# A chunk's triangular system solved in two steps of 64 tokens, without the last level of the inverse

## What is computed

```python
def _wkv_step(S, inp):
    r, w, k, v, a, b = inp
    sa = jnp.einsum('bhvk,bhk->bhv', S, a)
    S = S * w[:, :, None, :] + sa[..., None] * b[:, :, None, :] + v[..., None] * k[:, :, None, :]
    return S, jnp.einsum('bhvk,bhk->bhv', S, r)
...
S_T, y = lax.scan(_wkv_step, wkv0.astype(jnp.float32),
                  (tm(r), tm(decay), tm(k), tm(v), tm(-kk), tm(kk * a)))
```

## Time and profile before

| | before |
|---|---|
| median of the runs | 3294.47 us |
| span of the profiled execution | 3295.0 us |
| TensorE busy (products) | 3173.8 us, 96% |
| VectorE busy | 1845.3 us, 56% |
| ScalarE busy | 1332.7 us, 40% |
| GpSimd busy | 1201.8 us, 36% |
| mean granted TensorE clock | 0.991 |
| chunk stage, chunks 0 to 7 | about 1870 to 2402 us |
| one chunk of 1 to 6 | 66.5 us |

### The profile page before, as it was taken

The page is one execution under the profiler, slowest core; times in us unless marked ns, Lnnn a source line. Parts: engine busy times, 40 slices in busy tenths (PEclk is TensorE's granted clock), DMA queues, the critical chain, the costliest instruction groups (busy, mean ns, idle before and its releaser), DMA issues.

```text
span 3295.0 us, 69900 instructions
## 1 busy us (share of the span) xinstructions
PE 3173.8 (96%) x25744; PEld 2881.1 (87%) x25744; DVE 1845.3 (56%) x3147; ACT 1332.7 (40%) x2785; POOL 1201.8 (36%) x841
## 2 busy tenths in 40 slices
PE   8999999999999999999999999999999999999998
PEld 5688887787999999997899887878788899999998
DVE  3466663226444478857303377777744644458885
ACT  2244445512544533322213365565521355443332
POOL 0000000010766777721222222223223276677771
PEclk9999999999999999999999999999999999999999
DMA  3122224500544544422213201110152154554442
GB/s 113 43 79 65 71 74 147 180 13 20 159 155 157 187 138 137 139 96 75 84 53 114 99 14 34 33 40 27 29 179 45 50 161 158 158 186 141 140 140 77
DMA packets 306260, 330.39 MB, mean 100 GB/s; under 512 B 54350, under 2 KB 287745, under 8 KB 305954
## 3 DMA queue, kind: packets, MB, share of 16 engines
q1 hardware_dynamic: 300178, 308.64, 29.6%
q0 software_dynamic: 5904, 19.21, 1.8%
HBM read 232.05 MB, written 116.16 MB: 106 GB/s over the span
## 4 chain that ended last, share of the span: by engine, by line
PE 72%; DVE 8%; PEld 6%; issue 4%; POOL 3%; ACT 2%; SPq 2%; DMA 1%; DVEq 0%; PEldq 0%; ACTq 0%; POOLq 0%
PE bank L651 69%; PEld bank L651 6%; PE bank L659 4%; DVE arena L3605 1%; SPq L1769 1%; POOL wloA L2085 1%; DVE hT L3676 1%; POOL arena L2085 1%; POOL wloS L2085 1%; SPq L1710 0%; SPq L1764 0%; DVE arena L3058 0%; DVE arena L3622 0%; DVE arena L3166 0%; DVE fb L3310 0%
## 5 line engine op out<-in xcount | busy, mean ns | idle before, releaser
L651 PE MATMUL bank<-arena 128*32 128x128 f32 (+19 forms) x7390 | 947.8, 316 | 35.5 <-DVE hT L3676 12.9
L651 PEld LDWEIGHTS bank<-arena 128*128 128x128 f32 (+9 forms) x7390 | 734.8, 165 | 220.4 <-issue 36.8
L2302 ACT COPY arena<-bank 128x512 f32<-128x512 f32 (+14 forms) x527 | 235.0, 484 | 633.1 <-PE bank L651 430.4
L2085 POOL TENSOR_TENSOR arena<-arena 128x512 f32<-128x512 f32 x120 | 164.8, 1373 | 599.2 <-PE bank L651 366.9
L2525 ACT ACTIVATE whiS<-arena 128x512 fp32r<-128x512 f32 x180 | 113.0, 628 | 406.2 <-POOL arena L2085 390.7
L2085 POOL TENSOR_TENSOR wloA<-arena,whiA 128x512 fp32r<-128x512 f32 x180 | 261.4, 1466 | 13.4 <-ACT whiA L2522 13.4
L2085 POOL TENSOR_TENSOR wloS<-arena,whiS 128x512 fp32r<-128x512 f32 x180 | 238.7, 1340 | 49.1 <-ACT whiS L2525 49.1
L3471 DVE TENSOR_TENSOR hT<-hT,bank 128x536 f32<-128x536 f32 x280 | 197.6, 706 | 80.9 <-PE bank L651 80.4
L659 PE MATMUL bank<-table,arena 128*128 128x128 f32 (+5 forms) x1422 | 180.0, 268 | 29.1 <-DVE arena L3178 13.1
L651 PE MATMUL bank<-hiT,whiS 128*128 128x268 f32 x768 | 199.9, 288 | 5.3 <-DVE loT L3310 3.7
L3315 DVE TENSOR_TENSOR arena<-std,bank 128x268 f32<-128x268 f32 x192 | 80.4, 432 | 217.6 <-PE bank L651 206.3
(11 more groups left out here) (320 smaller groups left out, 8536.4 us busy)
## 6 DMA issues: line engine op xcount, KB each, us to landing
u_scratch<-arena SPq DMA_DIRECT2D x480, 134.0 KB, 1.8
arena<-in_ffn_w_up SPq DMA_DIRECT2D x64, 512.0 KB, 4.1
arena<-u_scratch SPq DMA_DIRECT2D x56, 536.0 KB, 5.0
arena<-in_ffn_w_down SPq DMA_DIRECT2D x112, 256.0 KB, 4.3
arena<-u_scratch SPq DMA_DIRECT2D x56, 402.0 KB, 5.9
arena<-past_scratch SPq DMA_DIRECT2D x32, 640.0 KB, 7.2
past_scratch<-in_cache_kv_latent SPq DMA_DIRECT2D x128, 128.0 KB, 2.4
past_scratch<-in_cache_k_rope SPq DMA_DIRECT2D x128, 32.0 KB, 2.2
```

The source lines that it names most:

```text
L651: return pe.matmul(out, lhsT, rhs, start=first, stop=last, skip_group_check=group)
L2085: return pool.tensor_tensor(out, a, b, op)
L2302: lane.do(act.copy(dst, b if view is None else view(b)), ring.drained)
```

## The change

The inverse stops at blocks of 64 tokens, so `level_64` and its three copies go. `solved` takes the place of `level_64`, `first_sums` and the first product of `finals`. It sums the right-hand side of the upper 64 tokens in one bank (`top`) and that of the lower 64 in another (`low`), solves the upper 64 with the upper block of XT, subtracts their part from the lower right-hand side by further products into `low`, and solves the lower 64. ScalarE copies P1 and SA each in two halves of 64 partitions, four copies in a row. On TensorE the filler `keep_busy` ahead of three steps goes, `key_sums` and `before(1)` move behind the upper solve, and one `keep_busy(rv)` stands behind the correction. On ScalarE `norms` and `deviations` (first half) and `diagonals` (second half) now stand behind all four copies.

```diff
+                def solved(d, fillers):
+                    upper, lower = slice(0, RN), slice(RN, P)
                     s_b.wait(pe, c)
-                    b = ra.bank()
+                    low = ra.bank(ahead=2)
+                    top = ra.bank(free=True)
                     for k in range(4):
-                        mm(b[:, k * P:(k + 1) * P], ar[:, 4 * d + k, 0, :], Sm[:, 4 * d + k, :], k == 0, False, True)
+                        for rows, out in ((upper, top), (lower, low)):
+                            mm(out[rows, k * P:(k + 1) * P], ar[:, 4 * d + k, 0, rows], Sm[:, 4 * d + k, :], k == 0, False, True)
+
+                    def value_sums(rows, out, depth, last):
+                        for j in range(8):
+                            h = 8 * d + j
+                            ins = mm(out[rows, j * RN:(j + 1) * RN], NR[0:depth, j * 2 * P + rows.start:j * 2 * P + rows.stop],
+                                     v[0:depth, h * RN:(h + 1) * RN], False, last and j == 7, True)
+                        return ins
+
+                    ra.done(value_sums(upper, top, RN, True))
+                    top_at = ra.filled.n
+                    value_sums(lower, low, P, False)
+                    b = narrow(ra, top_at)
+                    for j in range(8):
+                        ins = mm(b[upper, j * RN:(j + 1) * RN], XT[upper, j * P:j * P + RN], P1[upper, j * RN:(j + 1) * RN], True, True)
+                    ra.done(ins)
+                    fillers[0]()
+                    apart(ra.drained, ra.filled.value())
                     for j in range(8):
                         h = 8 * d + j
+                        ins = mm(low[lower, j * RN:(j + 1) * RN], ma[upper, h * P + RN:(h + 1) * P], SA[upper, j * RN:(j + 1) * RN],
+                                 False, j == 7, True)
                     ra.done(ins)
+                    low_at = ra.filled.n
+                    fillers[1]()
+                    b = narrow(ra, low_at)
+                    for j in range(8):
+                        ins = mm(b[lower, j * RN:(j + 1) * RN], XT[lower, j * P + RN:(j + 1) * P], P1[lower, j * RN:(j + 1) * RN], True, True)
+                    ra.done(ins)
 ...
                 def finals(d, taken, stated):
-                    keep_busy(ra)
-                    ra.wait_drained()
-                    b = ra.bank()
-                    for j in range(8):
-                        ins = mm(b[:, j * RN:(j + 1) * RN], XT[:, j * P:(j + 1) * P],
-                                 P1[:, j * RN:(j + 1) * RN], True, True)
-                    ra.done(ins)
                     sa_at = ra.filled.n
 ...
-                level_64(0, ma, [when(prepare, lambda: key_sums(c + 1, wn)), lambda: first_sums(0), nothing])
+                solved(0, [when(prepare, lambda: key_sums(c + 1, wn)), lambda: keep_busy(rv)])
 ...
-                level_64(1, ma, [nothing, lambda: first_sums(1), when(prepare, lambda: before(1))])
+                solved(1, [when(prepare, lambda: before(1)), lambda: keep_busy(rv)])
 ...
+            def rows_out(dst, rows, scale=1.0):
                 b = ring.bank()
+                lane.do(act.activation(dst[rows, :], b[rows, :], ACT.Copy, scale=scale), ring.drained)
+
+            def solved(others):
+                upper, lower = slice(0, RN), slice(RN, P)
+                rows_out(P1, upper)
+                rows_out(SA, upper, -1.0)
+                others()
+                rows_out(P1, lower)
+                rows_out(SA, lower, -1.0)
 ...
-                take_turned()
-                take_w_64()
+                solved(lambda: None)
                 if prepare:
                     norms(c + 1, wn)
                 if finish:
                     deviations(c - 1, P)
-                take(P1, P, 512)
-                take_x_64()
-                negated(SA, P, 512)
 ...
-                take_turned()
+                solved(lambda: None)
                 if wn == TAIL:
                     diagonals_tail()
                 elif prepare:
                     diagonals(c + 1, MA[1 - par])
-                take_w_64()
-                take(P1, P, 512)
-                take_x_64()
-                negated(SA, P, 512)
```

More of the change, by code:

```diff
@@ L1416, in level_32 @@
                 ra.done(ins)
-            def level_64(d, ma, fillers):
-                crossed_at = ra.filled.n
-                fillers[2]()
-                keep_busy(ra)
-                b = narrow(ra, crossed_at)
-                for j in range(8):
-                    ins = turn(b[0:64, j * 64:(j + 1) * 64], XT[0:64, j * P:j * P + 64], 64)
-                ra.done(ins)
[L1427 to L1440, removed]
@@ L1442, in chunk @@
             def chunk(c, par, nth, finish=True, prepare=True, wn=P):
                 ar, v, ma = AR[par], vt[par], MA[par]
-                def first_sums(d):
+                def solved(d, fillers):
+                    upper, lower = slice(0, RN), slice(RN, P)
                     s_b.wait(pe, c)
-                    b = ra.bank()
+                    low = ra.bank(ahead=2)
+                    top = ra.bank(free=True)
                     for k in range(4):
-                        mm(b[:, k * P:(k + 1) * P], ar[:, 4 * d + k, 0, :], Sm[:, 4 * d + k, :], k == 0, False, True)
+                        for rows, out in ((upper, top), (lower, low)):
[14 more added lines that the diff above has]
+                    fillers[0]()
+                    assert ra.filled.n == top_at + 1
+                    apart(ra.drained, ra.filled.value())
@@ L1452, in first_sums @@
                     for j in range(8):
                         h = 8 * d + j
-                        ins = mm(b[:, j * RN:(j + 1) * RN], NR[:, j * 2 * P:j * 2 * P + P],
-                                 v[:, h * RN:(h + 1) * RN], False, j == 7, True)
+                        ins = mm(low[lower, j * RN:(j + 1) * RN], ma[upper, h * P + RN:(h + 1) * P], SA[upper, j * RN:(j + 1) * RN],
+                                 False, j == 7, True)
+                    ra.done(ins)
+                    low_at = ra.filled.n
@@ L2836, in take_x_32 @@
                 lane.do(ins, ring.drained)
-            def take_turned():
-                take(XW6[0:64, :], 64, 512)
-            def take_w_64():
+            def rows_out(dst, rows, scale=1.0):
                 b = ring.bank()
[L2843 to L2847, removed]
+                lane.do(act.activation(dst[rows, :], b[rows, :], ACT.Copy, scale=scale), ring.drained)
[6 more added lines that the diff above has]
+                rows_out(SA, lower, -1.0)
             def key_factors(c, w):
```

## The result

| | before | after |
|---|---|---|
| median of the runs | 3294.95 us (4 runs) | 3382.32 us (4 runs, 3381.07 to 3384.50) |
| ratio to before, 95% interval | | 1.0263 (1.0248 to 1.0277) |
| span of the profiled execution | 3295.0 us | 3382.7 us |
| mean granted TensorE clock | 0.991 | 0.971 |
| full chunk | 66.5 us | 78.5 us |

What follows compares the result with a forecast made beforehand. VectorE's chain, almost level with TensorE's, has only 1.1 us slack per chunk, which decides. Six full chunks at 7.9 + 3.8 give 70, chunk 0 +3.7, chunk 7 +5: +79 on 3294.5, so 3373.5 us; range 3322 to 3396.

Steps and rivals of the forecast that it cites:

- A: The forecast itself: late diagonals, GpSimd collisions and the lower clock together, 3373 us; chance 0.50.
- TensorE's path: Solve steps after each half's last `level_32` product: the split solve lets TensorE's state product start 2.3 us earlier per half.
- Rival D: Half-width pairs don't overlap in the columns and lower value sums cost 1.90: 26 us more, 3400; chance 0.11.
- (a) diagonals: Second half, ScalarE: `diagonals` behind four copies starts `low_inverses` 11.65 us after the last `level_32` product, not 5.5.
- (b) roots: First half, ScalarE: `norms` and `deviations` behind SA lower leave 0.8 of TensorE's 2.3 us gain at `new_taken`.
- (c) GpSimd of the sum: Late group norm on GpSimd blocks VectorE's additions and scan: first half's last `level_32` product to second-half masks, 21.9 becomes 24.5.
- Rival C: Neither GpSimd collisions nor lower clock: +4.5 us per chunk, 3328 us; chance 0.13.
- The clock: Lower TensorE clock for about 5 us behind each of two idle times per chunk: +3.8 us per chunk.
- Rival B: Fillers hold the clock up or its cost is hidden under the masks: 3349 us; chance 0.17.
- Rival E: TensorE's path sets the end, VectorE's does not: 2.3 us gained in each of 16 halves, 3258 us; chance 0.06.

Runs made afterwards that it cites:

- e6: The kernel before, with only ScalarE's `diagonals` in the second half moved behind the copy of SA: 3370.7 us, ratio 1.0223.
- e5: The changed kernel in its own order, with GpSimd's group norm cut to 16 of 1024 columns: 3336.6 us, ratio 1.0120.
- e4: The changed kernel with 13 and 8 more filler products in TensorE's two long idle times per chunk: 3356.5 us, ratio 1.0190.
- e8: The kernel before without the three fillers per half that the change removes: 3335.6 us, ratio 1.0127.
- e1: The changed kernel with the second half's order undone (`before(1)` ahead of the solve, `diagonals` behind the copy of P1 upper): 3359.3 us, ratio 1.0191.
- e3: The changed kernel with the order of both halves undone (`diagonals`, `norms` and `deviations` early), split solve kept: 3342.8 us, ratio 1.0143.

## Why the prediction was right

Forecast 3373.5, measured 3382.3, in the range; the mechanism was the forecast one (A). By its steps, with the numbers of the chunk shown above:

- *TensorE's path.* State sums 1.09 (said 1.1), lower value sums as the 64x64 ones, SA at X + 8.6 (8.8). Rival D falls with them. One term was wrongly put at nothing, though it is small: the changes between 64-row and 128-row products do cost. In the trace of after, single products with 64 columns start 0.06 us apart within a group and 0.15 where the shape changes, so each of the four changes in a half takes about 0.1 us.
- *(a) diagonals.* `low_inverses` at Q + 11.5 (11.65), Q to L 23.4 (23.4). e6 isolates it.
- *(b) roots and (c) GpSimd of the sum.* `new_taken` at X + 12.5 (12.8), M at X + 24.1 (24.5). The order in which the two engines take turns was the one forecast, and the scan does wait. It took 3.24 us, against 2.28 in e5. Rival C falls. The page SBUF — State Buffer of the Trainium skill (section Who interferes with whom) says that a VectorE instruction with two SBUF inputs contends with a GpSimd instruction that reads SBUF; by these two numbers that holds for the scan too.
- *The clock.* L to X 15.4 (13.5 + 1.9), M to Q 15.6 (13.0 + 1.9). Against e4 that is 4.7 us (2.2 and 2.5), where I had 3.8. Idle times 7.60 and 4.69 (7.4 and 5). I had the lower clock last about 5 us of work behind each; at L it was 5.5, but at M 9.8 (granted clock 0.50 from 2214.3 to 2224.5). Rival B falls.
- *Rival E* falls by e6: 8.5 us of delay cost 8.7 per chunk.

A full chunk came out at 78.5 against 78.1. That it is so near is in part luck: at full clock it lost 7.3 us, not 7.9, and the lower clock took 4.7, not 3.8. One sign came out otherwise: TensorE was busy for 81% of the chunk, not for less than 75%; products at the lower clock last longer. The 9 us that were missing lie mostly elsewhere. By the starts of `new_taken` the six full chunks cost 72.0 more (said 70), chunk 0 4.8 (3.7), chunk 7 10.9 (5), and what follows the chunks 3.8 (nothing). Against that, the profiled run of after reached the stage 3.7 us earlier, which the change can't explain. Sum 87.8, the spans differ by 87.7. The step that was mis-sized is chunk 7: I had let it gain in its first half, and it gained 0.4 up to `new_taken`; but from there to Q it lost 3.8, with the lower clock behind an idle time of 3.0 us, and from Q to its end 7.5, where I had taken 6 less 1.2 of slack. Why the part behind the chunks costs 3.8 us was not tried; in the 48 us behind the last `new_taken` the mean granted clock was 0.77, against 0.86 before.

What the forecast didn't see is how near the old kernel stood to the same loss. I had taken the removed fillers for free, as their times lay under waits. In the order of the change they are: e4 fills only the two long idle times, leaves the removed fillers out, and has the mean granted clock of before again (0.991). In the old order e8 prices them at 39 us. And e1 and e3, which move the queue entries back, open waits that nothing fills. And I had no notion that undoing both orders would leave a kernel slower than before: e3's expectation made that mistake once more, with "no idle time above 2 us".

## What to carry to other kernels

Where engines run their lists in order, a step is paid for by what stands behind it. A shorter chain on TensorE brought SA 2.4 to 2.5 us earlier per half, and three entries queued behind its copies made the chunk 7.3 us longer even at full clock (e4); look up each moved entry's consumer on every engine before pricing the products. Products whose result nobody takes are not free to remove: fill the waits that a new order opens before judging it. And price two engines' elementwise work by when they meet, not only by how long each takes alone: a step that comes late can meet an operation that it used to pass (e3).

## What the runs showed of the hardware

- The granted clock fell from 2.4 to 1.2 GHz behind waits of TensorE as short as 0.87 and 0.75 us, 2 us apart, in e8, and behind one of 1.89 us in e1 and e3; the same product group then takes 1.97 instead of 1.11 us. It doesn't fall each time: the same two waits one chunk later in e8 left it up, and so did four of six waits of 1.7 us in e4. In e8 one chunk in two is 5 to 7 us longer though its work is the same.
- A VectorE operation with both operands in SBUF and a GpSimd one take turns, whole operations at a time, and both get longer: 5.10 us instead of 1.42 for two additions, 2.68 instead of 2.35 for a GpSimd operation. The ends fit this: an addition (0.69 alone) ends 0.55 us behind the GpSimd operation that it met, and the scan (2.28 alone) 2.15 behind. A copy of 8 columns within SBUF waits as well (1.75 instead of 0.17 us in e3). Operations that read PSUM pass untouched (1.27 against 1.28 us).
- A change between 128x64 and 64x64 products leaves no idle time in the timeline, as the modelled ends overlap, but it isn't free: in after the next product starts 0.15 us behind the last one instead of 0.06. Between groups of one shape (128x128 with 128 columns, then with 64) no such step stands in the trace of before: 0.11 us, as within a group.
